# Filler matmuls at the seams between the stages of a six-stage kernel (1 core, Trainium2)

## Chip, cores and metric

The kernel is one program on one core of a Trainium2 chip. The metric is the device time of one execution in microseconds (us). A matmul engine (TensorE, PE in the profile), a vector engine (VectorE, DVE), an activation engine (ScalarE, ACT), a general engine (GpSimd, POOL) and a queue for transfers (SyncE, SP) run their own instruction streams and wait for one another by semaphores.

## What is computed

The input is 256 tokens of 1024 features in float32. Six stages follow one another, each needing the whole result of the one before. In the reference, cut to its skeleton:

```python
# first block: two layers, residual factor DN_ALPHA, layer norm after each sum
h = layer_norm(DN_ALPHA * h + mixer_ab(h, ...), ln_g[0, 0], ln_b[0, 0])    # stage ab
h = layer_norm(DN_ALPHA * h + peer(h, ...), ln_g[0, 1], ln_b[0, 1])        # stage peer0
h = layer_norm(DN_ALPHA * h + mixer_c(h, ...), ln_g[1, 0], ln_b[1, 0])     # stage c
h = layer_norm(DN_ALPHA * h + peer(h, ...), ln_g[1, 1], ln_b[1, 1])        # stage peer1
# second block: 16 meta tokens are put ahead, RMS norm ahead of each part
h = h + hybrid_mixer(rmsnorm(h, g_mix), ...)                               # stage s
h = h + peer_ffn(rmsnorm(h, g_ffn), ...)                                   # stage peer2
out = rmsnorm(h, g_final)
```

A `peer` stage scores 8 heads of product keys, picks 16 of 16384 experts per head and token, and sums the chosen experts. The kernel does this densely: it multiplies all experts and weighs them with a gate matrix.

## The kernel before

**Tiling and staging.** All weights stream from memory as slabs of 128 x 1024 float32 (512 KB) through a ring of three buffers (`ring`). ScalarE copies a slab to a rounded high part (`w_hi`, line 771), and GpSimd or VectorE subtracts to get the low part (`w_lo`, line 478). TensorE then forms each product as three matmuls, high by high, low by high and high by low (lines 521 to 523). A "column" slab multiplies the transposed input `x_hi`, `x_lo` into one of three PSUM banks (`col`), 24 matmuls of 256 columns (`features`). A "row" slab adds into the four banks `acc`, 12 matmuls of 512 columns (`rows`), with its own activations `c_hi`, `c_lo`.

**The order of the work.** Every engine's program is written out by hand, one loop over the six stages, and semaphores order the engines among one another. Nothing is scheduled by a planner.

**A seam.** At the end of a stage the sums stand in `acc`. VectorE adds the residual (line 1031), centres (line 1063) and scales, with squares and roots on ScalarE (lines 828 and 811). The scaled quarters of the new `h` (a tile of 128 tokens by half of the features each) are written at line 1074 (layer norm) or line 1137 (RMS norm) and counted in the semaphore `h_part`. TensorE, in `transpose_x` (line 580), waits for each quarter and transposes it against the identity with four instructions. ScalarE copies each transposed quarter to `x_hi` (line 800), VectorE subtracts for `x_lo` (line 1015), and the next stage's first column slab begins when two quarters of `x_lo` are there (`x_ready`). Stage `s` has 16 meta tokens more, with 8 small transposes at line 586 and a last subtraction at line 1020. From the end of the last row slab to the first `h_part`, TensorE has nothing to do.

**The start.** There is no stage before `ab`: TensorE waits for the identity and for `x` (`const`, `xload`), transposes it, and waits for the first slabs. Between the first three slabs and the fourth, the queue of transfers carries the constants of stage `ab`.

Of the kernel before, what the change touches and what calls it, by code (L numbers as in the profile page):

```python
# [20 lines left out]
BF16 = mybir.dt.bfloat16  # L21
# [5 lines left out]
P = 128  # L27
# [3 lines left out]
NT = T // P  # L31
# [43 lines left out]

PARTS_OF = {"ab": ("in", "wide", "out"), "c": ("in", "wide", "gate", "out"), "s": ("in", "gate", "conv", "out")}
RMS_AFTER = ("s", "peer2")
STAGES = ("ab", "peer0", "c", "peer1", "s", "peer2")
STAGE_OF = {f"{x}_{part}": x for x in ("ab", "c", "s") for part in ("in", "wide", "gate", "conv", "out")} | {
    f"{x}{n}": f"peer{n}" for x in ("wq", "u", "v") for n in range(3)}  # L80
# [229 lines left out]
def view(t, at, *shape, p=P):  # L310

    n = int(np.prod(shape))
    v = t[0:p, at:at + n]
    if len(shape) == 1:
        return v
    names = "abcd"[:len(shape)]
    sizes = dict(zip(names[1:], shape[1:], strict=True))
    return v.rearrange(f"p ({' '.join(names)}) -> p {' '.join(names)}", **sizes)
# [195 lines left out]
class Tensor:  # L514
# [45 lines left out]
    def rows(self, s, y_hi, y_lo, start, stop):  # L560
# [8 lines left out]
                                         skip_group_check=True)  # L569
        ins.then_inc(k.used, 1)  # L570

    def transpose_x(self, src, meta, parts):

        k, pe = self.k, self.pe
        for t in range(NT):
            for half in range(2):
                if parts:
                    pe.wait_ge(k.h_part, parts - 4 + 2 * t + half + 1)
                for c in range(4):
                    ins = pe.transpose(k.acc[t * 2 + half][:, c * P:(c + 1) * P],  # L580
                                       src[t][:, (4 * half + c) * P:(4 * half + c + 1) * P], k.ident[:, :])
                ins.then_inc(k.xt, 1)
        if meta is not None:
            self.w.next(k.meta_ready)
            for c in range(DC):
                ins = pe.transpose(k.misc[:, c * META:(c + 1) * META], meta[:, c * P:(c + 1) * P],
                                   k.ident[0:META, 0:META])
            ins.then_inc(k.xt, 1)
# [145 lines left out]
def tensor_program(k, pe):  # L734
    e = Tensor(k, pe)
    pe.wait_ge(k.const, 32)
    pe.wait_ge(k.xload, 16 * NT)
    for name in k.stages:
        if name == "s" or k.after_s(name):
            src = [view(k.big, NORMED + t * D, D) for t in range(NT)]  # L740
        else:
            src = [k.h[:, t, :] for t in range(NT)]
        meta = view(k.big, NORMED + 2 * D, D, p=META) if name == "s" else None
        e.transpose_x(src, meta, k.parts_before(name))
        if name == "s":
            e.w.next(k.x_ready, 5)
        if name[:4] == "peer":
            e.peer(int(name[4]))
        else:
            MIXERS[name](k).tensor(e)  # L750
# [5 lines left out]
class Scalar:  # L756
# [87 lines left out]
    def finish(self, name, end):  # L844
# [8 lines left out]
        self.split_lead(Slab(end))  # L853
        if name in RMS_AFTER:
            for t in range(NT):
# [509 lines left out]
def vector_program(k, dve):  # L1365
# [7 lines left out]
    for name in k.stages:  # L1373
# [7 lines left out]
        else:  # L1381
            MIXERS[name](k).vector(e)
            last = k.first[f"{name}_out"] + k.count[f"{name}_out"] - 1
        if name in RMS_AFTER:
            e.finish_rms(name, last)
# [1128 lines left out]
def build(nc, dram, out, stages):  # L2514
    with ExitStack() as ctx:
        k = Kernel(nc, ctx, dram, out, stages)
        block = ctx.enter_context(nc.Block())

        @block.sync
        def _(sp):  # L2520
            sync_program(k, sp)

        @block.gpsimd
        def _(pool):
            gpsimd_program(k, pool)

        @block.scalar
        def _(act):
            scalar_program(k, act)

        @block.tensor
        def _(pe):
            tensor_program(k, pe)

        @block.vector
        def _(dve):
            vector_program(k, dve)
# [96 lines left out]
```

## Time and profile before

| | |
|---|---|
| time, median of 3 executions | 3044.0 us (3039.75 to 3045.32) |
| the profiled execution's own time | 3041.95 us |
| its span, first to last instruction | 3040.2 us |
| mean TensorE clock granted | 0.986 of full |
| PE busy | 2950.7 us (97%) |
| DVE, ACT, POOL busy | 69%, 52%, 31% |
| bytes moved | 508.62 MB, mean 167 GB/s |

The span is what the profile's positions refer to; the time of an execution is a little longer than its span (1.75 us here). The granted clock is 1.0 where TensorE runs at 2.4 GHz and 0.5 where it runs at 1.2 GHz.

### The profile page before, as it was taken

To read this page: it belongs to the slowest core of one execution; us is meant where nothing else is said; L and a number is where in the kernel's file an instruction comes from. 1 tells how busy PE (TensorE), PEld (TensorE's weight loads), DVE (VectorE), ACT (ScalarE), POOL (GpSimd) and SP (SyncE) were. 2 spreads that over 40 slices of the span, in tenths; PEclk is the share of its full clock that TensorE was granted. 3 is DMA by queue.
4 is the path that set the end of the run, shared out by engine and by line. 5 is a ranking of instruction groups with operands and counts; after the bars stand their busy time and mean duration, and the time that the engine had idled before them with its cause. 6 is when DMAs were issued, how large, how long until landed. Compare 5 with 4: busy or idle time off the path is not lost.

```text
span 3040.2 us, 66263 instructions
## 1 busy us (share of the span) xinstructions
PE 2950.7 (97%) x22893; PEld 2687.5 (88%) x22893; DVE 2086.7 (69%) x4319; ACT 1580.0 (52%) x2614; POOL 940.8 (31%) x378
## 2 busy tenths in 40 slices
PE   7899999999999989999999999899999999999998
PEld 6799999888888879999998888788799999988887
DVE  4369488888555654948888865575429488788755
ACT  3444444677555444444457755564544444477654
POOL 5589600000004747980000000155779820000000
PEclk9999999999999999999999999899999999999999
DMA  5455555555664425555555566444555555555554
GB/s 189 141 171 180 180 159 165 166 166 166 219 193 158 139 92 172 186 184 157 164 167 166 166 213 195 142 132 125 152 161 179 187 166 160 169 161 166 186 193 159
DMA packets 142701, 508.62 MB, mean 167 GB/s; under 512 B 17136, under 2 KB 18160, under 8 KB 142592
## 3 DMA queue, kind: packets, MB, share of 16 engines
q1 hardware_dynamic: 142592, 507.16, 52.2%
q8 instruction: 69, 1.13, 0.2%
q14 instruction: 40, 0.33, 0.0%
HBM read 506.05 MB, written 1.05 MB: 167 GB/s over the span
## 4 chain that ended last, share of the span: by engine, by line
PE 87%; DVE 6%; ACT 3%; POOL 2%; issue 1%; DMA 1%; SPq 0%; DVEq 0%; ACTq 0%; POOLq 0%
PE col L521 14%; PE col L523 14%; PE col L522 14%; PE acc L521 13%; PE acc L523 12%; PE acc L522 12%; POOL w_lo L478 2%; PE acc L644 2%; PE col L644 2%; ACT w_hi L771 1%; PE acc L604 1%; DMA ring<-in_ab_in 1%; DVE work L1829 0%; DVE mask_i L1271 0%; ACT work L828 0%
## 5 line engine op out<-in xcount | busy, mean ns | idle before, releaser
L478 POOL TENSOR_TENSOR w_lo<-ring,w_hi 128x1024 fp32r<-128x1024 f32 x374 | 940.6, 2525 | 1509.6 <-ACT w_hi L771 1508.8
L771 ACT ACTIVATE w_hi<-ring 128x1024 fp32r<-128x1024 f32 x941 | 993.5, 1056 | 558.8 <-PE acc L523 460.3
L521 PE MATMUL col<-x_hi,w_hi 128*128 128x256 f32 (+1 forms) x3976 | 1133.4, 285 | 13.4 <-DVE x_lo L1015 8.7
L522 PE MATMUL col<-x_lo,w_hi 128*128 128x256 f32 (+1 forms) x3976 | 1122.6, 282 | 0.0
L523 PE MATMUL col<-x_hi,w_lo 128*128 128x256 f32 (+1 forms) x3976 | 1121.8, 282 | 0.0
L478 DVE TENSOR_TENSOR w_lo<-ring,w_hi 128x1024 fp32r<-128x1024 f32 x567 | 693.3, 1223 | 263.6 <-ACT w_hi L771 262.3
L521 PEld LDWEIGHTS col<-x_hi,w_hi 128*128 128x128 f32 x3976 | 754.7, 190 | 18.2 <-issue 12.9
L523 PEld LDWEIGHTS col<-x_hi,w_lo 128*128 128x128 f32 x3976 | 755.6, 190 | 0.0
L522 PEld LDWEIGHTS col<-x_lo,w_hi 128*128 128x128 f32 x3976 | 752.1, 189 | 0.7
L521 PE MATMUL acc<-w_hi,c_hi 128*128 128x512 f32 x1664 | 662.1, 398 | 10.6 <-DVE c_lo L1155 8.7
L523 PE MATMUL acc<-w_hi,c_lo 128*128 128x512 f32 x1664 | 651.1, 391 | 0.0
L522 PE MATMUL acc<-w_lo,c_hi 128*128 128x512 f32 x1664 | 649.9, 391 | 0.0
L778 ACT ACTIVATE work<-col 128x256 f32 (+1 forms) x464 | 178.8, 385 | 774.3 <-PE col L523 774.3
L521 PEld LDWEIGHTS acc<-w_hi,c_hi 128*128 128x128 f32 x1664 | 313.8, 189 | 76.6 <-DVE c_lo L1155 9.8
L523 PEld LDWEIGHTS acc<-w_hi,c_lo 128*128 128x128 f32 x1664 | 313.8, 189 | 67.7
L522 PEld LDWEIGHTS acc<-w_lo,c_hi 128*128 128x128 f32 x1664 | 314.3, 189 | 62.5
L1281 DVE TENSOR_TENSOR gated_onehot_i<-mask_i,pairs_of_gate 128x768 bf16<-128x768 bf16 x384 | 216.9, 565 | 12.2
L1162 DVE TENSOR_TENSOR c_lo<-work,c_hi 128x256 fp32r<-128x256 f32 x384 | 160.3, 419 | 1.4 <-ACT c_hi L932 1.4
L1271 DVE TENSOR_TENSOR mask_i<-iota_bf,pairs_of_i_i 128x256 bf16<-128x256 bf16 x384 | 127.1, 331 | 43.9 <-DVE gated_onehot_i L1281 41.0
L932 ACT ACTIVATE c_hi<-work 128x256 fp32r (+1 forms) x384 | 153.3, 401 | 5.9 <-DVE work L1291 5.9
L1169 DVE MAX8 work<-work 128x8 f32<-128x128 f32 (+1 forms) x144 | 35.4, 323 | 168.1 <-ACT work L888 167.8
L1276 DVE TENSOR_TENSOR onehot_i<-iota_bf,pairs_of_i_i 128x512 bf16<-128x512 bf16 x288 | 122.8, 426 | 0.0
(284 smaller groups left out, 2072.6 us busy)
## 6 DMA issues: line engine op xcount, KB each, us to landing
ring<-in_u SPq DMA_DIRECT2D x384, 512.0 KB, 3.4
ring<-in_v SPq DMA_DIRECT2D x384, 512.0 KB, 3.7
ring<-in_wq SPq DMA_DIRECT2D x48, 512.0 KB, 3.4
ring<-in_s_in SPq DMA_DIRECT2D x21, 512.0 KB, 3.7
ring<-in_c_in SPq DMA_DIRECT2D x16, 512.0 KB, 3.3
ring<-in_s_out SPq DMA_DIRECT2D x16, 512.0 KB, 3.7
ring<-in_s_gate SPq DMA_DIRECT2D x12, 512.0 KB, 3.7
ring<-in_s_conv SPq DMA_DIRECT2D x12, 512.0 KB, 3.7
```

The lines of the kernel that those rows point to most:

```text
L478: eng.tensor_tensor(k.w_lo[s.slot][:, :], k.ring[s.slot][:, :], k.w_hi[s.slot][:, :].bitcast(F32), ALU.subtract).then_inc(k.lo[s.slot], 1)
L521: pe.matmul(out, a[0], b[0], start=start, stop=False, **kw)
L522: pe.matmul(out, a[0], b[1], start=False, stop=False, **kw)
L523: return pe.matmul(out, a[1], b[0], start=False, stop=stop, **kw)
L644: ins = pe.matmul(banks[b.slot][:, t * EARLY:(t + 1) * EARLY], k.oh1[:, b.base % 2, t, :], k.oh2[:, b.base % 2, n, t, :], start=n == 0, st ...
L771: act.activation(k.w_hi[s.slot][:, :], k.ring[s.slot][:, :], ACT.Copy).then_inc(k.hi[s.slot], 1)
L778: act.activation(dst, src, func).then_inc(k.evac, 1)
L932: act.activation(k.c_hi[s.slot][:, :], act_of[:, s.index(values), :], ACT.Copy).then_inc(k.coef_h, 1)
L1162: dve.tensor_tensor(k.c_lo[s.slot][:, :], src, k.c_hi[s.slot][:, :].bitcast(F32), ALU.subtract).then_inc(k.coef[s.slot], 1)
L1271: dve.tensor_tensor(mask, pairs[:, at // 2:(at + EARLY) // 2, :].unsqueeze(1).to_broadcast(shape), k.i2[:, tokens, :].unsqueeze(2).to_broa ...
L1276: dve.tensor_tensor(k.oh1[:, slot, :, :].rearrange("p t (i two) -> p t i two", two=2), pairs.unsqueeze(1).to_broadcast(shape), k.i1[:, tok ...
L1281: dve.tensor_tensor(k.oh2[:, slot, :, :, :].rearrange("p n t (i two) -> p n t i two", two=2), mask.unsqueeze(1).to_broadcast(shape), k.gat ...
```

## The change

A new method issues `n` matmuls of the identity by itself, read as bf16 (256 bf16 columns of a 128 x 128 float32 tile), into the bank `col[2]`, which no one reads before it is written again. They wait for nothing and nothing waits for them. A table gives how many stand before and after the transposes of each stage. Once per program the wait for `x` moves behind the first group.

```diff
+BUSY = {"ab": (24, 50), "peer0": (40, 0), "c": (40, 0), "peer1": (40, 0), "s": (80, 0), "peer2": (20, 0)}
...
+    def keep_busy(self, n):
+
+        k = self.k
+        ones = k.ident[:, :].bitcast(BF16)
+        for _ in range(n):
+            self.pe.matmul(k.col[2][:, 0:2 * P], ones[:, 0:P], ones, start=True, stop=True)
+
...
     pe.wait_ge(k.const, 32)
-    pe.wait_ge(k.xload, 16 * NT)
     for name in k.stages:
...
+        before, after = BUSY[name]
+        e.keep_busy(before)
+        if name == k.stages[0]:
+            pe.wait_ge(k.xload, 16 * NT)
         e.transpose_x(src, meta, k.parts_before(name))
+        e.keep_busy(after)
```

On TensorE, at the seam from `ab` to `peer0`, the program before has the last row slab's matmuls, then the 16 transposes, then the first column slab (`acc` are the row banks, `c_hi` and `c_lo` the row activations):

```order
L522 MATMUL acc<-w_lo,c_hi 128x512
L523 MATMUL acc<-w_hi,c_lo 128x512
L580 MATMUL acc<-ident,h_tok 128x128 x16
L521 MATMUL col<-x_hi,w_hi 128x256
L522 MATMUL col<-x_lo,w_hi 128x256
```

and the changed program has, at the same place (all lines are numbered one to eight higher there, so 521 is now 522 and 580 is 588):

```order
L523 MATMUL acc<-w_lo,c_hi 128x512
L524 MATMUL acc<-w_hi,c_lo 128x512
L578 MATMUL col<-ident 128x256 x40
L588 MATMUL acc<-ident,h_tok 128x128 x16
L522 MATMUL col<-x_hi,w_hi 128x256
```

Only the row of line 578 is new; it stands behind the last real matmul and ahead of the transposes that wait for `h_part`. The seams into `c` and `peer1` read the same. On TensorE at the very start of the changed program:

```order
L578 MATMUL col<-ident 128x256 x24
L588 MATMUL acc<-ident,h_tok 128x128 x16
L578 MATMUL col<-ident 128x256 x50
L522 MATMUL col<-x_hi,w_hi 128x256
```

Here the two new groups stand on both sides of the transposes, and before there was only the second row. Into `s` (`misc` is the bank of the meta tokens' transposes) the changed TensorE program reads:

```order
L578 MATMUL col<-ident 128x256 x80
L588 MATMUL acc<-ident,work 128x128 x16
L594 MATMUL misc<-ident,work 128x16 x8
L522 MATMUL col<-x_hi,w_hi 128x272
```

and again the first row is all that is new. The other engines' programs are unchanged.

## Rows read from the trace of the kernel before

**Rows 1.** The page's line of busy time: engine, us, share, instructions.
```profile
PE 2950.7 (97%) x22893; PEld 2687.5 (88%) x22893; DVE 2086.7 (69%) x4319; ACT 1580.0 (52%) x2614; POOL 940.8 (31%) x378
```

**Rows 2.** Waits of TensorE: waiting line <- releaser: total us, times, longest.
```profile
PE acc L580 <- DVE h_tok L1074: 15.0, 3, 5.0
PE acc L580 <- DVE work L1137: 14.7, 4, 9.9
PE col L521 <- DVE x_lo L1015: 8.7, 5, 4.5
```

**Rows 3.** Windows at the layer-norm seams: stretch, length, busy PE PEld DVE ACT POOL, clock, DMA.
```profile
112.15:117.16 5.01, 0.00 (x1) 0.00 (x1) 4.82 (x12) 3.23 (x9) 0.00 (x0) 0.99 0.17 66
117.16:121.49 4.33, 3.58 (x17) 3.31 (x17) 3.52 (x7) 2.86 (x6) 2.37 (x1) 0.61 0.24 39
121.49:124.49 3.00, 3.00 (x25) 3.00 (x26) 1.05 (x2) 0.84 (x1) 2.09 (x1) 1.00 0.57 206
943.27:948.27 5.00, 0.00 (x1) 0.00 (x0) 4.81 (x12) 3.23 (x9) 0.00 (x0) 0.83 0.20 81
948.27:952.60 4.33, 3.67 (x16) 3.31 (x17) 3.52 (x7) 2.77 (x6) 2.37 (x1) 0.50 0.13 15
952.60:956.78 4.18, 4.18 (x19) 4.18 (x20) 3.43 (x7) 2.87 (x4) 2.38 (x1) 0.50 0.30 114
1124.39:1128.71 4.32, 3.43 (x16) 3.22 (x17) 3.51 (x7) 2.99 (x6) 2.37 (x1) 0.65 0.25 38
```

**Rows 4.** Windows at the seams into s and peer2; two timeline rows into peer2.
```profile
1949.54:1959.93 10.39, 0.45 (x2) 0.03 (x2) 8.71 (x22) 8.13 (x21) 4.63 (x3) 0.69 0.18 57
1959.93:1966.75 6.82, 4.91 (x25) 4.07 (x25) 5.23 (x12) 4.47 (x12) 0.47 (x1) 0.50 0.43 144
1966.75:1970.54 3.79, 3.79 (x17) 3.79 (x17) 0.40 (x3) 0.00 (x0) 0.00 (x0) 0.50 0.00 0
2201.84:2208.49 6.65, 3.64 (x16) 2.63 (x17) 4.02 (x9) 5.82 (x13) 3.20 (x2) 0.56 0.14 39
2208.49:2212.88 4.39, 4.39 (x20) 4.39 (x21) 1.05 (x2) 0.00 (x0) 1.49 (x1) 0.50 0.71 236
...
2201.84 1.68 PE L580 MATMUL acc<-ident,work 128*128 128x128 f32 x8 [2.65 <-DVE work L1137]
...
2206.05 2.06 ACT L800 ACTIVATE x_hi<-acc 128x512 fp32r<-128x512 f32 x4
```

**Rows 5.** Timeline: 24 gate matmuls in bf16 and 12 transposes, both at full clock.
```profile
391.52 0.87 PE L644 MATMUL acc<-gated_onehot_i,onehot_i 128*128 128x64 bf16 x24
...
1089.18 1.53 PE L1730 MATMUL col<-ident,work 128*128 128x128 f32 x12 [0.83 <-ACT work L778]
```

**Rows 6.** Timeline of the seam from ab to peer0: start, us, instruction, idle before.
```profile
117.16 3.58 PE L580 MATMUL acc<-ident,h_tok 128*128 128x128 f32 x16 [5.01 <-DVE h_tok L1074]
121.49 0.36 PE L521 MATMUL col<-x_hi,w_hi 128*128 128x256 f32 x1 [0.75 <-DVE x_lo L1015]
...
117.87 1.41 DVE L1074 SCALAR_TENSOR_TENSOR h_tok<-acc,small,work 128x512 f32<-128x512 f32 x2
120.65 1.89 DVE L1015 TENSOR_TENSOR x_lo<-acc,x_hi 128x512 fp32r<-128x512 f32 x3 [0.78 <-ACT x_hi L800]
```

**Rows 7.** Timeline of GpSimd at the start of stage c (the fourth slab).
```profile
959.04 2.40 POOL L478 TENSOR_TENSOR w_lo<-ring,w_hi 128x1024 fp32r<-128x1024 f32 x1 [3.06 <-ACT w_hi L771]
```

**Rows 8.** Start of stage ab: TensorE's first slab and fourth slab, and a window.
```profile
15.13 0.55 PE L521 MATMUL col<-x_hi,w_hi 128*128 128x256 f32 x1 [4.54 <-DVE x_lo L1015]
25.99 0.35 PE L521 MATMUL col<-x_hi,w_hi 128*128 128x256 f32 x1 [0.80 <-POOL w_lo L478]
...
16.00:17.00 1.00, 1.00 (x7) 1.00 (x7) 0.18 (x1) 0.00 (x0) 1.00 (x1) 0.50 1.06 414
```

**Rows 9.** Windows inside stage ab: a wait, and the matmuls behind it.
```profile
76.97:79.00 2.03, 0.02 (x1) 0.00 (x0) 0.00 (x0) 1.97 (x3) 1.66 (x2) 1.00 0.45 182
79.00:82.00 3.00, 2.89 (x15) 2.89 (x16) 0.52 (x1) 2.43 (x4) 1.51 (x1) 0.59 0.63 198
```

## The prediction

> **What bounds the kernel now.** I read four views, from coarse to fine. The page's busy line says that TensorE works 97% of the span [rows 1], so what can be won lies in its few waits and in stretches at half clock. The view of waits then names them: the transposes at the head of a stage wait 15.0 us over three layer-norm seams and 14.7 us over the RMS-norm seams, and first slabs wait 8.7 us for `x_lo` [rows 2]. All of these are waits for VectorE and ScalarE, which filler matmuls don't shorten. The windows show the clock. In the 5.0 us without a matmul before each layer-norm seam's transposes the granted clock falls from full (2.4 GHz) to half (1.2 GHz), at the very end of the wait into `peer0` (mean 0.99) and earlier into `c` (mean 0.83). Then the transposes run at half clock, and into `c` so do the first 19 matmuls of the stage, up to 956.78 [rows 3]. The RMS-norm seams look worse: 3.79 us of half-clock matmuls into `s` and 4.39 us into `peer2` [rows 4]. So the kernel loses, besides the waits, some microseconds per seam to a slow clock, and that alone is what the change can reach.
>
> **What the fillers cost.** The trace has no 256-column bf16 matmul. From above: 24 gate matmuls of 64 bf16 columns with their weight loads take 0.87 us, 0.036 us each [rows 5], and 192 columns more at 2.4 GHz add 0.080, which makes 0.116 us. The fp32r matmuls of 256 columns take 3.00 / 25 = 0.12 us each at full clock [rows 3]. From below: 256 columns at 2.4 GHz are 0.107 us. I take 0.116. At half clock it is twice the columns' time, 0.213 at least (19 fp32r matmuls in 4.18 us are 0.22 [rows 3]). So 40 fillers last 4.6 us against a wait of 5.0 us [rows 3], 80 last 9.3 us against 10.4, and 20 last 2.3 us against 2.65 [rows 4]. The fillers end before `h_part` comes by 0.4, 1.1 and 0.3 us, so they cost nothing themselves. The cover is thin: a layer-norm seam pays every nanosecond by which one filler exceeds 0.125 us.
>
> **A layer-norm seam, step by step** (into `peer0`; the others read alike). With the clock kept up, four transposes take 4 x 1.53 / 12 = 0.5 us instead of 0.9 [rows 5, 6]. Transposes also wait for each quarter of `h`. VectorE writes the third and fourth from 117.87 on in 1.41 us, so the third is there at about 118.6. Its transposes end at 119.1 instead of about 120.0, ScalarE's copy (0.6 us) ends at 119.7, and VectorE, which waited 0.78 us for it before 120.65 [rows 6], no longer waits. The first slab waits for that subtraction, so it starts 0.78 us earlier. That is all that the transposes' speed gives: of 1.8 us saved on TensorE, the rest was behind VectorE's own pace anyway. Into `peer0` and `peer1` the clock of the profiled execution had already risen within the transposes (means 0.61 and 0.65, and 1.00 behind them [rows 3]), so these two seams give 0.8 us each.
>
> **Into c** there is more. 19 matmuls at half clock take 4.18 us [rows 3], and at 0.12 us they take 2.3: 1.9 us less. Late next is the fourth slab. GpSimd finishes its low part at 959.04 + 2.40 = 961.44 [rows 7]. The chain of small operations behind it on VectorE and ScalarE starts from the same `x_lo`, so it moves up by 0.78 too, to 960.66. TensorE would be through three slabs at 951.82 + 72 x 0.12 = 960.46 and waits 0.2 us. The seam gives 0.8 + 1.9 - 0.2 = 2.5 us.
>
> **Into s and peer2** the fillers cover only the first wait. Behind it lie 6.82 us and 6.65 us until the first slab, in which TensorE at half clock is busy 4.91 and 3.64 us [rows 4], and at full clock about half of that, with pauses near 2 us between the bursts. Does the clock last through? Inside stage `ab` it fell within the matmuls that followed a single wait of 2.0 us (mean 0.59 over 79 to 82 [rows 9]). So here it falls again, before the first slab or just behind it, and it comes back as late as now. Into `peer2` the transposes' speed does not matter either: ScalarE copies all four quarters in one go from 2206.05 [rows 4], after its own slab work. I give `peer2` nothing and `s` 0.3 us for faster transposes in its last tile.
>
> **At the start** the 24 fillers ahead (5.1 us at half clock) lie in the wait for `x`, and what they might push back ends at the same place as the rest. The 50 behind the transposes last 5.8 us at full clock against a wait of 4.54 us: the first slab would start 1.3 us late. In return it does not run at half clock (0.50 at 16 to 17 us [rows 8]), which is worth about 14 x 0.1 = 1.4 us. And whatever is won or lost here meets the fourth slab, which comes from a transfer behind the constants; TensorE waits 0.80 us for it at 25.99 [rows 8]. Net 0. Should all 50 run at half clock (10.7 us, 6.1 late), 0.8 us of that is hidden and some 4 us are lost.
>
> **The sum.** 0.8 + 2.5 + 0.8 + 0.3 + 0 + 0 = 4.4 us. The profiled execution took 3041.95 us, so 3037.6. That execution is 2 us below the median of 3044.0, and I do not add these 2 us back. Where the clock rises behind a layer-norm seam changes between three seams of the same program: within the transposes at two, 4.18 us into the matmuls at the third [rows 3]. So it is chance per seam, worth 0 to 1.9 us, and slower executions of the kernel before plausibly lost it at more seams. With fillers no seam depends on it. Against the median the gain is then 4.4 + 2.0 = 6.4 us.
>
> **The rule that speaks against this.** The row first: between 112.15 and 121.49 the only instructions of TensorE are the 16 transposes, and the clock rises while they run (mean 0.61 from 117.16, full behind) [rows 3], so transposes do raise the clock. The Trainium skill, "TensorE: Matmul & The Clock Gate", Part 4, says that the clock gate does not engage for transpose-mode matmuls, which don't count as busy the same way. By that rule the fillers' effect would lapse before the first slab, and the sum would be near 0; the trace disagrees with it.
>
> **The rivals.**
> - *The clock lapses within the transposes* (the rule above, as a mechanism of this kernel). At full clock the transposes are busy 1.8 of 4.3 us, much thinner than the dense 3.58 us of now. If the clock falls about when the first slab begins, each of three seams keeps 0.8 us and runs some 4 us of matmuls slowly, which costs 1.9. Into `peer0` and `peer1` that is new (+1.1 each), into `c` it is what stands now (-0.8). With `s` it sums to +1.1: 3043. For it: the single wait of 2.0 us that sufficed in [rows 9]. Against it: the longest pause in these seams would be about 0.9 us. Chance 0.15.
> - *The change does not do what it says*: the identity read as bf16 is nearly all zeros, and if that doesn't hold the clock, all is as before, 3040 to 3045. Against it: the gate matmuls, on one-hot operands nearly all zeros too, run through at full speed [rows 5]. Chance 0.10.
> - *It holds everywhere*: `s` and `peer2` also keep their clock, which gives 3.79 x 0.45 + 4.39 x 0.45 = 3.7 us more: 3034. Chance 0.12.
> - *The fillers outlast the wait* (the one that ends slower). Its place is ahead of the transposes: TensorE runs in order, so `h_part` arrives and finds it multiplying the identity. Each filler beyond 0.125 us delays three seams by 40 x the excess and `s` by 80 x the excess over 0.130. It eats the gain of 4.4 us at about 0.15 us per filler (3.0 + 1.6 us) and gives 3050, 0.2% above the median, at about 0.18 us. At half clock, 0.213, it would be 3.5 us at three seams and 6.6 at `s`: 3055. For it: margins of 0.4 us on a price that the trace only bounds. Against it: both bounds are below 0.125. Chance 0.05.
>
> The forecast has the remaining 0.58.
>
> **How the numbers follow.** A measurement of this kernel can tell about 0.2% (6 us) from no change. The forecast, 3037.6, stands at the edge of that against 3044.0, so it splits nearly evenly between faster and the same; the case of all seams is faster, the two without effect are the same, and the last is half slower. Faster 0.58 x 0.55 + 0.12 + a little = 0.45; slower 0.04; same 0.51. The range takes in the full hold, 3034, with the executions' own scatter of about 1 us below, and the two cases without gain up to 3043. The forecast's own range is 3035 to 3040.
>
> **What would show it.** In the profile after: the fillers at 0.107 to 0.12 us each; clock 1.00 through the layer-norm seams; each of these seams' first matmul 0.8 us sooner after the last row matmul; VectorE's 0.78 us wait before `x_lo` gone; clock 0.5 still in the first slabs of `s` and `peer2`; the wait for the fourth slab in `ab` longer than 0.80 us. Wrong would be a half clock in the first slab of `peer0`, `c` or `peer1`, or transposes that start with no wait behind the fillers.

## Result and the profile after

| | kernel before | changed kernel |
|---|---|---|
| median of 10 runs each, us | 3040.73 | 3046.47 |
| lowest to highest, us | 3036.16 to 3045.32 | 3040.64 to 3051.51 |
| profiled execution, us | 3041.95 | 3046.23 |

The ratio is 1.0022 with a 95% interval of 1.0012 to 1.0033: the changed kernel is slower by 0.2%, some 6 us. I had forecast 3037.6 us and a gain, and had given 0.04 to slower. Both kernels scatter by 9 to 11 us from run to run, which matters for all that follows.

The page of the changed kernel, TensorE's busy line and the queue that brings the instructions of the long programs (packets, MB, share of the DMA engines' time):

```profile
PE 2978.3 (98%) x23187; PEld 2708.2 (89%) x23187; DVE 2090.1 (69%) x4319; ACT 1580.2 (52%) x2614; POOL 941.9 (31%) x378
...
q8 instruction: 71, 1.16, 0.2%
```

Against [rows 1] there are 23187 - 22893 = 294 matmuls more, and nothing else of size. Queue 8, whose packets are of 16 KB, had 69 packets in the kernel before.

TensorE's waits in the changed kernel (who waits <- releaser: total us, times, longest):

```profile
PE acc L652 <- DVE gated_onehot_i L1293: 7.3, 3, 4.3
PE col L522 <- POOL w_lo L479: 6.7, 7, 2.3
PE col L522 <- DVE x_lo L1027: 5.0, 4, 2.5
PE acc L588 <- DVE work L1149: 4.8, 4, 1.6
PE acc L588 <- DVE h_tok L1086: 2.4, 6, 0.6
```

And the two of them that had been smaller in the kernel before:

```profile
PE acc L644 <- DVE gated_onehot_i L1281: 4.7, 3, 1.6
PE col L521 <- POOL w_lo L478: 3.4, 6, 1.3
```

The waits of [rows 2] shrank as they should (15.0 to 2.4, 14.7 to 4.8, 8.7 to 5.0 us; the rest is now fillers). Two others grew: for the gates in the peer stages (4.7 to 7.3 us) and for GpSimd's low part of the weights (3.4 to 6.7 us).

The windows at the layer-norm seams and into `s` and `peer2` (stretch, length, busy PE PEld DVE ACT POOL, granted clock, DMA share, GB/s):

```profile
118.28:121.95 3.67, 2.62 (x17) 1.70 (x17) 3.51 (x7) 2.95 (x6) 2.36 (x1) 1.00 0.13 26
...
948.50:952.18 3.68, 2.62 (x16) 1.71 (x17) 3.52 (x7) 2.95 (x6) 2.38 (x1) 1.00 0.00 0
952.18:956.00 3.82, 3.82 (x32) 3.82 (x33) 3.44 (x4) 2.02 (x2) 2.41 (x1) 1.00 0.41 137
...
1962.73:1969.55 6.82, 4.25 (x25) 3.34 (x25) 5.24 (x12) 4.47 (x12) 0.48 (x1) 0.68 0.40 129
1969.55:1973.00 3.45, 3.45 (x15) 3.45 (x16) 0.39 (x3) 0.00 (x0) 0.00 (x0) 0.50 0.03 5
...
2206.77:2213.42 6.65, 2.62 (x17) 1.71 (x17) 4.02 (x9) 5.82 (x13) 3.20 (x2) 1.00 0.16 39
2213.42:2218.00 4.58, 4.58 (x26) 4.58 (x27) 1.05 (x2) 0.00 (x0) 1.49 (x1) 0.63 0.72 224
```

Beside [rows 3], the transposes and the first slab of the layer-norm stages now run at clock 1.00 (2.4 GHz), and from the first transpose to the first slab it takes 3.67 us instead of 4.33. Into `s` that stretch is 6.82 us as in [rows 4] and the first slab runs at half clock again (0.50), and into `peer2` it is 6.65 us, also as in [rows 4], although the transposes there now run at full clock. So the fillers do hold the clock where I said, and the stretch is shorter where I said. The time is lost elsewhere.

The timeline of TensorE (start, us, what, and in brackets the wait ahead) at the start, into `peer0`, at the fourth slab of `c` and into `s`:

```profile
3.48 5.30 PE L578 MATMUL col<-ident 128*128 128x256 bf16 x24 [3.48 <-DMA work<-in_iota]
8.58 2.29 PE L588 MATMUL acc<-ident,h_tok 128*128 128x128 f32 x16
10.70 5.62 PE L578 MATMUL col<-ident 128*128 128x256 bf16 x50
16.08 0.36 PE L522 MATMUL col<-x_hi,w_hi 128*128 128x256 f32 x1
...
113.11 4.54 PE L578 MATMUL col<-ident 128*128 128x256 bf16 x40
118.28 0.44 PE L588 MATMUL acc<-ident,h_tok 128*128 128x128 f32 x2 [0.62 <-DVE h_tok L1086]
...
963.23 0.35 PE L522 MATMUL col<-x_hi,w_hi 128*128 128x256 f32 x1 [2.29 <-POOL w_lo L479]
...
1952.63 8.91 PE L578 MATMUL col<-ident 128*128 128x256 bf16 x80
1962.73 0.66 PE L588 MATMUL acc<-ident,work 128*128 128x128 f32 x4 [1.20 <-DVE work L1149]
```

40 fillers take 4.54 us and end 0.62 us before the transposes can start. At the fourth slab of `c` stands a wait of 2.29 us that the kernel before did not have.

**Where the time went.** I set every real matmul of one trace against the same one of the other, since both programs have the same 22893. Into `peer0`, the shorter stretch is there. In `c`, the changed kernel is 2.3 us ahead of the kernel before by the fourth slab, where the wait of 2.29 us takes all of it back. The largest step is in `peer1`: between 1342 and 1380 us the changed kernel loses 4.5 us, with no filler near. A smaller one, 2 us near 2000 and 2015 us in stage `s`, is not there in a second profile of the same program (e1 below). Here are the rows. Behind the routing transposes (line 634) the sync engine issues the 512 KB transfer of a slab. Its issue and the time to landing, and a packet of queue 8 found between 1344.2 and 1344.5, in the changed kernel:

```profile
q8 instruction: 1, 0.02, 25.3%
...
ring<-in_u SPq DMA_DIRECT2D x1, 512.0 KB, 5.0
```

the same transfer in the kernel before, where the packet of queue 8 comes at 1350.1, 2.7 us after the transfer has landed:

```profile
ring<-in_u SPq DMA_DIRECT2D x1, 512.0 KB, 3.1
```

What then follows on ScalarE, VectorE, GpSimd and TensorE, in the timelines of the changed kernel:

```profile
1347.75 1.06 ACT L783 ACTIVATE w_hi<-ring 128x1024 fp32r<-128x1024 f32 x1 [1.25 <-DMA ring<-in_u]
1348.72 0.36 ACT L929 ACTIVATE neg_i<-misc 128x256 f32<-128x256 f32 x1
...
1354.16 2.51 DVE L1265 TENSOR_TENSOR gated_onehot_i<-gated_onehot_i,pairs_of_gate 128x256 f32<-128x256 f32 x1
...
1367.21 0.55 DVE L1293 TENSOR_TENSOR gated_onehot_i<-mask_i,pairs_of_gate 128x768 bf16<-128x768 bf16 x1
...
1348.89 12.59 POOL L479 TENSOR_TENSOR w_lo<-ring,w_hi 128x1024 fp32r<-128x1024 f32 x5 [1.71 <-ACT w_hi L783]
...
1367.81 0.39 PE L652 MATMUL acc<-gated_onehot_i,onehot_i 128*128 128x64 bf16 x4 [4.32 <-DVE gated_onehot_i L1293]
```

its window behind the wait:

```profile
1367.81:1370.00 2.19, 2.19 (x19) 2.19 (x20) 1.61 (x5) 0.00 (x0) 0.00 (x0) 0.51 0.68 239
```

and in the kernel before:

```profile
1348.99 0.38 ACT L917 ACTIVATE neg_i<-misc 128x256 f32<-128x256 f32 x1
...
1354.80 0.42 DVE L1253 TENSOR_TENSOR gated_onehot_i<-gated_onehot_i,pairs_of_gate 128x256 f32<-128x256 f32 x1
...
1349.17 2.40 POOL L478 TENSOR_TENSOR w_lo<-ring,w_hi 128x1024 fp32r<-128x1024 f32 x1 [0.34 <-ACT w_hi L771]
1352.08 2.41 POOL L478 TENSOR_TENSOR w_lo<-ring,w_hi 128x1024 fp32r<-128x1024 f32 x1 [0.50 <-ACT w_hi L771]
...
1366.55 0.44 PE L644 MATMUL acc<-gated_onehot_i,onehot_i 128*128 128x64 bf16 x9 [1.42 <-DVE gated_onehot_i L1281]
```

Read it as a chain. The transfer lands 1.9 us later. ScalarE works in order and waits 1.25 us for it, and the small copy `neg_i` stands behind that slab: counted from the routing transposes (1342.4 and 1344.1 us) it starts at +6.3 instead of +4.9. Now GpSimd has five slabs to do in a row (12.59 us) instead of one or two at a time with pauses of 0.3 to 0.7 us between, and the operation of VectorE that took 0.42 us in such a pause takes 2.51 us beside it. So the gates come 2.9 us later, TensorE waits 4.32 us instead of 1.42, and in that pause its clock falls (0.51 over the next 2.19 us). One 16 KB packet of instructions at the wrong moment costs 4.5 us.

That was the theory after the result: **the fillers cost through the instructions that they add.** 294 matmuls are 588 instructions of TensorE, and where in the program queue 8 fetches its next block moves with their number. The rivals were that the fillers cost something by running (power, banks, a wait that they outlast), or that 6 us is chance between executions. The Trainium skill, "Runtime: NRT & Kernel Launch", section "Instruction fetch mechanics", says that each engine's sequencer fetches its instructions itself in blocks of 16 KB (256 instructions) over a DMA queue of its own, and that crossing a block's boundary is mostly hidden. The size agrees with the trace (1.16 MB / 71 packets). That it is hidden agrees for TensorE itself, whose idle time put down to issue is 0.7 us in all; it does not hold for the transfer beside it.

### The profile page after: what moved, and what is told of

The parts are those of the page before. It is cut to its first block, busy times and chain, and to the rows that moved or that the text cites. A ratio compares the mean times of both kernels' runs of the same rounds, so it can differ in the third digit from the quotient of the medians.

```text
span 3044.4 us, 66850 instructions
## 1 busy us (share of the span) xinstructions
PE 2978.3 (98%) x23187; PEld 2708.2 (89%) x23187; DVE 2090.1 (69%) x4319; ACT 1580.2 (52%) x2614; POOL 941.9 (31%) x378
## 3 DMA queue, kind: packets, MB, share of 16 engines
q8 instruction: 71, 1.16, 0.2%
## 4 chain that ended last, share of the span: by engine, by line
PE 86%; DVE 6%; ACT 3%; POOL 3%; issue 1%; DMA 1%; SPq 0%; ACTq 0%; DVEq 0%; POOLq 0%
PE col L522 14%; PE col L524 14%; PE col L523 14%; PE acc L522 13%; PE acc L524 12%; PE acc L523 12%; POOL w_lo L479 3%; PE acc L652 2%; PE col L652 2%; ACT w_hi L783 1%; PE acc L612 1%; DMA ring<-in_ab_in 1%; DVE work L1841 0%; DVE mask_i L1283 0%; ACT work L840 0%
## 5 line engine op out<-in xcount | busy, mean ns | idle before, releaser
L522 PEld LDWEIGHTS col<-x_hi,w_hi 128*128 128x128 f32 x3976 | 754.1, 190 | 17.3 <-issue 11.7
```

The lines of the kernel that those rows point to most:

```text
L522: pe.matmul(out, a[0], b[0], start=start, stop=False, **kw)
```

## Experiments

The thirteen traces answer more than their times, so here is one table ahead. For each peer stage: when the fetch of queue 8 starts, counted from the first routing transpose; when the slab transfer issued at +0.2 lands; when ScalarE's `neg_i` starts; what TensorE waits for gates in the stage; and the time from the first routing transpose to the 300th matmul behind it (all us, worked out from the traces' records).

| kernel, stage | fetch | landed | neg_i | gate waits | 300 matmuls |
|---|---|---|---|---|---|
| before, peer0 | +1.2 | +4.50 | +5.55 | 1.62 | 33.1 |
| before, peer1 | +6.0 | +3.33 | +4.93 | 1.42 | 32.9 |
| changed, peer0 | +1.18 | +4.28 | +5.33 | 1.37 | 32.9 |
| changed, peer1 | +1.84 | +5.25 | +6.30 | 4.32 | 37.4 |
| changed again, peer0 | +1.5 | +5.15 | +6.20 | 4.20 | 37.9 |
| changed again, peer1 | +2.17 | +5.30 | +6.35 | 4.37 | 37.9 |
| e3, peer0 | +1.18 | +4.32 | +5.37 | 1.64 | 33.2 |
| e3, peer2 | +1.28 | +5.20 | +6.25 | 4.26 | 37.2 |
| e5, peer0 | +1.47 | +4.68 | +5.73 | 3.96 | 37.6 |
| e5, peer1 | +2.09 | +5.35 | +6.40 | 4.27 | 37.5 |
| e6, peer0 | +1.18 | +4.44 | +5.49 | 1.65 | 33.2 |
| e6, peer1 | +1.78 | +4.94 | +5.99 | 4.15 | 37.7 |
| e7, peer0 | +1.24 | +4.53 | +5.58 | 1.63 | 33.1 |
| the other 26 | +3.5 and later | +3.3 to +3.7 | +4.9 | 1.35 to 1.63 | 32.9 to 33.2 |

Two remarks. The effect is a step: up to `neg_i` at +5.58 nothing is lost, from +5.73 on 4 to 5 us are, in seven of the 39 stages. The kernel before stands close to the step itself, in its `peer0`, so it may pay in some of the executions that were not profiled; that is not shown. And the late landing is one sixteenth of the transfer. A transfer counts up its semaphore sixteen times, once for each of the 16 DMA engines. In all twelve stages with a fetch at +1.2 to +2.2, fifteen of the sixteen counts are there by +3.3 to +3.7, as in a stage without a fetch, and one alone comes at +4.3 to +5.35.

Each experiment was timed against the kernel before on its own chip; that one's median was 3037.61 us for the first four runs, 3037.60 for the next four and 3040.71 for the last three.

**The changed kernel again** (e1).

> The changed kernel once more, unaltered. In its first profile it lost 4.5 us at one place outside the seams: the wait for the gated one-hots in stage peer1 was 4.32 us where the kernel before had 1.42, and the clock fell behind it. Theory A (that place is chance, and the seams give back what they win): the wait is back at 1.4 to 1.6 us here, the span is 3040 to 3042, and over the rounds the ratio is below 1.002. Theory B (the long wait belongs to the change, because stages start sooner and meet transfers and GpSimd in another phase): the wait is above 3 us again, the span near 3044, ratio 1.002 or more.

3047.72 us, ratio 1.0035 [1.0022, 1.0047]. So it is slower on a second chip too, and both intervals lie above 1. In its profiled execution the collision stands in two stages, `peer0` and `peer1`; in the first profile of the same program `peer0` had escaped it, with its fetch 0.3 us earlier against the transposes.

**The layer-norm seams alone** (e2).

```
-BUSY = {"ab": (24, 50), "peer0": (40, 0), "c": (40, 0), "peer1": (40, 0), "s": (80, 0), "peer2": (20, 0)}
+BUSY = {"ab": (0, 0), "peer0": (40, 0), "c": (40, 0), "peer1": (40, 0), "s": (0, 0), "peer2": (0, 0)}
```

> Fillers at the three layer-norm seams alone (40 each; none at the start, at s and at peer2). Theory A: each seam's first matmul comes 0.7 us sooner, the fourth slab of stage c waits above 2 us and takes c's gain back, so the time is 1 to 3 us below the kernel before. Theory B: the wait for the gated one-hots of peer1 is above 3 us and the time is 3 to 6 us above the kernel before. Theory C (the harm is at s and peer2): as A.

3034.16 us, ratio 0.9989 [0.9980, 0.9998]: 3.5 us faster than before, with the same fillers at the same seams as in the changed kernel. None of its three peer stages has a fetch before +7.9.

**s and peer2 alone** (e3): 80 fillers into `s`, 20 into `peer2`, none elsewhere.

> Fillers at the seams into s and peer2 alone (80 and 20). Theory A: no gain and no loss, within 1 us of the kernel before, since the clock falls behind the fillers anyway and the transposes are paced by VectorE. Theory C (the fillers there move the fall of the clock into the matmuls of stage s, whose half-clock stretches in the changed kernel were 1970 to 1975 and 2012 to 2016): 3 to 5 us above the kernel before. Theory B: as A.

3043.24 us, ratio 1.0019 [1.0009, 1.0028]. No gain at these seams, and a loss of 5.6 us between the medians. The profile shows 4.1 of it in `peer2`, where the fetch fell on +1.28 (+11.5 in the kernel before). That execution took 3037.39 us, one of the two fastest of twelve, so what the slower ones lost beside it is not seen.

**The start alone** (e4): 24 and 50 fillers in `ab`.

> Fillers at the start alone (24 and 50). All theories but one expect nothing, within 1 us: the fourth slab of stage ab waits for its transfer (1.04 us in the changed kernel). Theory D (the start moves the phase of everything that follows, above all of the chip's clock decisions, and the program's other waits happen to lie badly for it): 2 us or more above the kernel before.

3042.05 us, ratio 1.0013 [1.0004, 1.0021]. Slower, and no peer stage of its profile has a collision. Here the theory of the number fell short, and e10 below takes it up.

**All 294, each a quarter as wide** (e5). The instructions and their places are those of the changed kernel, but with 64 columns each TensorE is idle for most of every wait.

```
-            self.pe.matmul(k.col[2][:, 0:2 * P], ones[:, 0:P], ones, start=True, stop=True)
+            self.pe.matmul(k.col[2][:, 0:P // 2], ones[:, 0:P], ones[:, 0:P // 2], start=True, stop=True)
```

> All 294 fillers of the change, at the same places, but each of 64 columns: about 0.036 us each, so 40 last 1.4 us and don't hold the clock, while the program has exactly as many instructions. The traces show 16 KB instruction fetches whose place in the program moves with the fillers' number; where one falls 1.1 to 2.2 us behind the routing transposes of a peer stage, the slab transfer there lands at +4.3 to +5.3 us instead of +3.3 and the wait for the gates grows from 1.4 to up to 4.4 us. Theory C (instruction volume): fetches at peer0 +1.2 to +1.5 and peer1 +1.8 to +2.2 as in the changed kernel, a gate wait above 4 us at peer1, and a ratio of 1.002 to 1.005, since the layer-norm seams' gain is gone too. Theory E (the harm is in what the fillers execute): within 0.1% of the kernel before.

3045.37 us, ratio 1.0025 [1.0016, 1.0034]. A loss of this size is there while the fillers' work is down to a fraction: the added instructions alone are enough for it. That is not the same loss part by part, since the seams' gain and the start's cost are gone too. TensorE's largest waits in this kernel:

```profile
PE acc L588 <- DVE work L1149: 12.1, 4, 7.6
PE acc L588 <- DVE h_tok L1086: 11.5, 3, 3.8
PE acc L652 <- DVE gated_onehot_i L1293: 9.9, 4, 4.0
```

The first two are the seams' waits, nearly as long as in [rows 2]; the third holds the collisions in `peer0` and `peer1`, 4.5 us each by the table, 9 in sum against a measured 7.8.

**40 and then 74 short fillers at one seam** (e6, e7). The kernel before, with nothing added but short fillers into `peer1`:

```
+BUSY = {"ab": (0, 0), "peer0": (0, 0), "c": (0, 0), "peer1": (40, 0), "s": (0, 0), "peer2": (0, 0)}
```

and (74, 0) in the second.

> The kernel before with 40 fillers of 64 columns (1.4 us in a wait of 5.0) at the seam into peer1 alone. They move the fetch of peer1 from +6.0 to about +1.9 us. Theory C: slab landed at +4.3 to +5.3, gate wait above 4 us at peer1 and a half-clock stretch behind it, 3 to 5 us above the kernel before (ratio 1.001 to 1.0015). Theory E: gate wait 1.4 us, ratio 1.000.

> As e6_pad40 but with 74 fillers of 64 columns (2.7 us, still inside the wait): nearly twice the instructions. The fetches of peer1 and peer2 then lie at about +13 and +3.5 us, outside the harmful stretch. Theory C: gate waits 1.4 and 1.6 us, ratio within 0.0007 of 1, so less harm than with 40. A theory by which harm grows with the number of instructions expects more than in e6_pad40.

With 40: 3040.77 us, ratio 1.0009 [0.9999, 1.0019]. With 74: 3039.54 us, ratio 0.9998 [0.9990, 1.0007]. The times alone hardly separate the two. The traces do. The 33 us behind the routing transposes of `peer1`, with 40:

```profile
1343.60:1376.60 33.00, 28.85 (x245) 28.69 (x244) 22.17 (x22) 12.43 (x19) 22.52 (x10) 0.90 0.46 160
```

and with 74:

```profile
1342.20:1375.20 33.00, 31.63 (x304) 31.43 (x303) 25.74 (x31) 14.24 (x23) 22.48 (x10) 1.00 0.51 176
```

304 matmuls at clock 1.00 against 245 at 0.90, and the clean one is the kernel with *more* added instructions. The fetch behind `peer1`'s routing transposes moved from +6.0 to +1.8 with 40 fillers. With 74 no fetch is near: the last one ahead is at 1194.8 us, and the next comes at +13.4. These are single traces, but they tell the place of a fetch from the number of instructions as such.

**The changed kernel with its fetches moved** (e8). The fillers of the layer-norm seams, of `s` and the first 24 stay. The start's 50 become 90 short ones, and `peer2`'s 20 become 108 short ones, so that no fetch falls between +0.2 and +3 in a peer stage.

```
-BUSY = {"ab": (24, 50), "peer0": (40, 0), "c": (40, 0), "peer1": (40, 0), "s": (80, 0), "peer2": (20, 0)}
+BUSY = {"ab": (24, 0), "peer0": (40, 0), "c": (40, 0), "peer1": (40, 0), "s": (80, 0), "peer2": (0, 0)}
+MOVED = {"ab": (0, 90), "peer2": (108, 0)}
...
+        e.keep_busy(MOVED.get(name, (0, 0))[0], P // 2)
         e.transpose_x(src, meta, k.parts_before(name))
         e.keep_busy(after)
+        e.keep_busy(MOVED.get(name, (0, 0))[1], P // 2)
```

> The changed kernel with its fetches moved: the 50 fillers behind the first transposes become 90 of 64 columns, and the 20 of peer2 become 108 of 64 columns, so that peer0 and peer1 see 40 fillers' instructions more ahead of them and peer2 128 more, one fetch in all. Layer-norm seams and s keep their full fillers. Theory C: no fetch between +0.2 and +3 us at any of the three peers, gate waits 1.4 to 1.6 us, 5 to 9 us below the changed kernel and at or below the kernel before (ratio 0.998 to 1.001). Theory E: as the changed kernel, 1.002 to 1.0035.

3036.68 us, ratio 0.9993 [0.9984, 1.0002], with fetches at +11.7, +8.7 and +5.9. It has 128 fillers more than the changed kernel, and by the ratios (1.0022 and 1.0035, on other chips) it is 9 to 13 us faster. The start also changed in this kernel, so not all of that is the fetches'.

**Is c worth its fillers?** (e9, with e11). e9 is e2 with the 40 fillers of `c` 64 columns wide; e11 is e2 once more, as its companion.

```
-        e.keep_busy(before)
+        e.keep_busy(before, P // 2 if name == "c" else 2 * P)
```

> The fillers of the layer-norm seams alone, and those of stage c with 64 columns each in place of 256: the same instructions at the same places, but TensorE idles through most of c's wait. If what the fillers win at c is all given back at its fourth slab (a wait of 2.3 us there, in the place of 19 matmuls at half clock), the profile shows half clock behind c's transposes and no wait at the fourth slab, and the time is within 1 us of the kernel with all three seams held, next to it in the same comparison. The rival, that c is worth the 2.5 us of my sum: 2.5 us slower than that kernel.

> The kernel with the 3 x 40 fillers of the layer-norm seams alone, once more, as the companion of the one with c's fillers short. It measured 0.9989 [0.998, 0.9998]; if that was more than luck it comes out at 0.9985 to 0.9995 again, with all gate waits of the peer stages below 1.7 us. The rival, luck: 0.9997 or more.

e11: 3037.22 us, ratio 0.9986 [0.9976, 0.9996], so the gain of the three seams stands (3.5 us between the medians both times). e9: 3039.86 us, ratio 0.9998 [0.9989, 1.0006], 2.6 us more than e11, though the intervals overlap. By my expectation that is the rival's number, and the trace is not as I expected either. Its windows over the transposes of `c`, the first three slabs, the wait for the fourth, and a stretch behind it:

```profile
945.74:950.06 4.32, 3.40 (x16) 3.19 (x17) 3.51 (x7) 3.01 (x6) 2.37 (x1) 0.65 0.09 28
950.06:958.50 8.44, 8.43 (x71) 8.44 (x72) 5.81 (x9) 4.81 (x7) 2.39 (x1) 1.00 0.34 112
958.50:961.03 2.53, 0.29 (x3) 0.10 (x2) 0.00 (x0) 2.40 (x4) 2.49 (x2) 1.00 0.00 0
...
962.50:965.80 3.30, 3.30 (x17) 3.30 (x17) 0.00 (x0) 0.38 (x2) 3.05 (x2) 0.50 0.72 242
```

The clock had come back within the transposes this time, so the first slabs ran at full clock without the fillers' help, met the fourth slab's wait (2.25 us), and the clock fell behind that wait. The fourth slab starts 14.7 to 14.8 us behind the first transpose in the kernel before and in all five traces with full fillers at `c`, and 14.4 to 15.3 in the seven others without. What delays it where the clock is full is shown under "Into c" below. The 414th matmul from the first transpose comes at +54.9 to +55.0 in four of those five and at +56.5 in one, and at +54.6 to +57.0 (mean 55.5) in the eight without. By these records full fillers at `c` win 0.3 us on average; by the times of e9 and e11 they could win up to 2.6. Both are within what chance does here, and this stays open.

**The start with short fillers** (e10): e4 with 64 columns each.

> The 74 fillers of the start alone, with 64 columns each. The same 74 with 256 columns measured 3042.05 us, ratio 1.0013, with every gate wait of the peer stages short. If what costs there is the added instructions (the fetch that moves from 26 to 18 us, in between the transfers of the constants), this is the same, 1.001 to 1.002. If it is TensorE's time, 50 full fillers that outlast the wait for the first slab, it is gone: 0.999 to 1.0003, and the first slab starts at 14 to 15 us.

3039.86 us, ratio 1.0000 [0.9991, 1.0009], with its first fetch at 17.7 us, close to e4's (18.3). By the expectation it is not the number but TensorE's time, though the two intervals overlap and the two were timed on different chips. TensorE's timeline at the start, e4 first:

```profile
4.15 5.28 PE L578 MATMUL col<-ident 128*128 128x256 bf16 x24 [4.15 <-DMA work<-in_iota]
9.24 1.93 PE L588 MATMUL acc<-ident,h_tok 128*128 128x128 f32 x16
```

and e10:

```profile
6.75 3.67 PE L588 MATMUL acc<-ident,h_tok 128*128 128x128 f32 x16 [2.26 <-DMA h_tok<-in_x]
...
13.99 0.38 PE L522 MATMUL col<-x_hi,w_hi 128*128 128x256 f32 x1 [1.89 <-DVE x_lo L1027]
...
25.46 0.36 PE L522 MATMUL col<-x_hi,w_hi 128*128 128x256 f32 x1 [1.21 <-POOL w_lo L479]
```

The wide fillers outlast both waits: in e10 `x` is there at 6.75 while in e4 the transposes start at 9.24, and the first slab, which in e10 starts at 13.99, starts at 16.39 in e4. But nothing of that is left at the fourth slab. e10 waits 1.21 us for it and starts it at 25.46, e4 runs its first slabs at full clock and starts it at 24.99, with no wait, and the kernel before starts it at 25.99 [rows 8]. By the first transpose of `peer0` e4 is 1.1 us behind e10 and 0.6 us behind the kernel before (117.72 against 116.64 and 117.16), and at the end of the span 0.6 us behind the kernel before. So the 4.4 us between the medians of e4 and the kernel before (0.0013 of the time by the ratio) are not placed: the profiled executions don't show them at the start or anywhere else.

## Why the prediction was wrong

**The step that failed** is the sentence "The fillers end before `h_part` comes by 0.4, 1.1 and 0.3 us, so they cost nothing themselves." The margins were right. But I asked only what the fillers do while they run, and left out the term for what they are: 588 instructions that have to be fetched, and whose fetches meet the transfers of the slabs. That term is 4.0 to 5.0 us for each peer stage in which a fetch starts +1.3 to +2.2 us behind the routing transposes. The changed kernel pays it in `peer1` in both profiles, and in `peer0` in one of two. None of my four rivals named it, and the slower side had 0.04 for all causes together.

**What the fillers cost.** I took 0.116 us each; 4.54 / 40 = 0.114 and 8.91 / 80 = 0.111 were measured. They outlast none of the five later waits (0.62, 0.61, 0.60, 1.20 and 0.45 us are left). Right. A slip in the rival of outlasting fillers: at 0.18 us per filler its own terms give 120 x 0.055 + 80 x 0.050 = 10.6 us and 3048; the 3050 that it names belong to about 0.19. It changes no chance.

**A layer-norm seam.** Clock 1.00 through all three: right, in every profile with full fillers there. 0.78 us sooner: 4.33 - 3.67 = 0.66 us, in all 17 such seams of the thirteen traces (3.67 or 3.68), against 4.13 to 4.33 in the 22 without. VectorE's wait of 0.78 us is gone: four subtractions now follow in one row,

```profile
120.31 2.69 DVE L1027 TENSOR_TENSOR x_lo<-acc,x_hi 128x512 fp32r<-128x512 f32 x4
```

so that step was right and its size 0.1 us too large. What I undervalued is `peer1`. In five of seven traces without full fillers there, the clock was still half behind the first slab for some 4 us, as in this row of e3:

```profile
1121.20:1125.10 3.90, 3.90 (x18) 3.90 (x19) 1.05 (x2) 0.93 (x1) 2.37 (x1) 0.51 0.45 156
```

which costs about 2 us more; in all six with them it was 1.00. I had read one trace, where the clock had come back in time, and had put this to chance "worth 0 to 1.9 us". (That it was 1.00 behind `peer1`'s transposes I gave as [rows 3], which end before; the trace does have it.) Into `peer0` it did not happen in any of seven.

**Into c.** Here the term was mis-sized: I had TensorE wait 0.2 us for the fourth slab, and it waits 2.29 to 2.34 us in all five traces. The step that failed is "it moves up by 0.78 too, to 960.66". I let the chain of small operations keep its length, and it got longer. The changed kernel, GpSimd and VectorE:

```profile
952.99 2.41 POOL L479 TENSOR_TENSOR w_lo<-ring,w_hi 128x1024 fp32r<-128x1024 f32 x1 [1.68 <-ACT w_hi L783]
...
953.15 2.27 DVE L1817 TENSOR_TENSOR work<-work 128x8 f32<-128x8 f32 x1
```

and the kernel before:

```profile
953.60 2.38 POOL L478 TENSOR_TENSOR w_lo<-ring,w_hi 128x1024 fp32r<-128x1024 f32 x1 [2.54 <-ACT w_hi L771]
...
953.57 0.16 DVE L1805 TENSOR_TENSOR work<-work 128x8 f32<-128x8 f32 x1
```

The first small operation, 8 elements wide, took 0.16 us when it started 0.03 us ahead of GpSimd's subtraction, and takes 2.27 us when it starts 0.16 us behind it. Those 2.1 us pass down the chain: counted from the first transpose, GpSimd ends the low part of the fourth slab at +14.6 instead of +13.2, where +12.4 was forecast. It is the same in all thirteen traces. In seven the first slabs of `c` run at full clock, GpSimd starts first, the small operation takes 2.1 to 2.3 us and TensorE waits 2.1 to 2.3 us for the fourth slab (e4 and e9 among them, without full fillers at `c`). In the other six the first ones run at half clock, the operation takes 0.16 us and there is no wait. So TensorE's faster slabs win nothing. Of 2.5 us forecast, 0 to 0.3 are seen in the traces (and up to 2.6 in one pair of times).

**The sum of the three** was 4.1 us, and e2 and e11 measured 3.5 each. That agreement is partly luck: `c` gave less and `peer1` more than their terms.

**s and peer2.** Right in the main: the first slab into `s` is at half clock (0.50), the one into `peer2` mostly (a mean of 0.63 over 4.58 us, 0.50 over 4.39 before), and nothing is gained in `peer2`. Its transposes do run at full clock (1.00), and it brings nothing, since the first slab waits for ScalarE and VectorE, as I had it. The 0.3 us for `s` are not in the changed kernel's first profile (6.82 us to the first slab, as before), but in the three others with its 80 fillers (6.50, 6.35 and 6.37).

**At the start** I had net 0. The full-width fillers hold back the first slab, 16.08 us instead of 15.13. I had the 1.3 us that the 50 outlast the wait, but not that the 24 (5.3 us at half clock, from 3.48 on) outlast the one for `x`; I had written that "what they might push back ends at the same place". In the traces it does end at the same place: the fourth slab starts at 25.88 us in the changed kernel and at 25.99 in the kernel before. The wait for it is longer in the changed kernel's first profile, 1.04 us against 0.80, as forecast, but e1 and e4, with the same start, have none. By the times the term was not 0 but 4.4 us (e4), and where they are lost stays open.

**The rule on transposes** that I weighed (the Trainium skill, "TensorE: Matmul & The Clock Gate", Part 4: the clock gate does not engage for transposes) was rightly set aside for this kernel: the clock rises within the transposes with the last filler 3.82 us ahead of them (e9, 0.65 over 945.74 to 950.06 and 1.00 behind), and behind the fillers the transposes of the three seams run at 1.00 throughout, with 2.62 us busy in 3.67, and the slabs behind them too.

**The ledger** in medians: three seams -3.5, the start +4.4 (e4), one collision +4.5, a second one in some executions up to +4.6. That makes 5.4 to 10.0 us, against 5.7 and 10.1 us measured in the two comparisons. The sum comes out, but not every term of it is explained: the start's share is a difference of medians that no profile shows, and how often the second collision happens is known from two profiles alone.

## What to carry to other kernels

An instruction that does nothing useful still has to be fetched, and on a kernel whose transfers are tight the question is not how many instructions are added but which transfer the next block of instructions then meets. So after such a change look first at the stages that it did not touch, and compare two versions that differ by instructions alone (short dummies in the place of long ones) before giving a price to what the instructions do.

A faster engine also shifts when its neighbours meet. At the seams where a slab's data was ready the fillers gave 0.7 us and a safe clock. In `c` they brought GpSimd's subtraction just ahead of a small operation of VectorE that TensorE's fourth slab depends on, instead of just behind it, and lost there what they had won. And one trace shows one draw of a clock that comes back early or late; the same seam should be read in several.

## What was not expected of the hardware

- A fetch of 16 KB of instructions that starts 1.0 to 1.9 us after a 512 KB transfer on 16 DMA engines was issued made that transfer land 4.4 to 5.1 us after its issue instead of 3.1. A 16 KB packet is 1/32 of its bytes. Fifteen of the transfer's sixteen counts come in time and one alone is late, which fits one DMA engine whose share waits behind the packet.
- Some of VectorE's operations take 2.1 to 2.6 us when they start while a GpSimd operation runs, whatever their own size: 2.51 us instead of 0.42 for 256 elements, and 2.27 instead of 0.16 for 8. In `peer1` this turned 1.4 us of delay into 2.9, and in `c` it took back the whole gain.
- Another two-way draw: the first wait of a later part of stage `ab` (TensorE for VectorE's pool mixer) is 4.74 us in eight traces and 2.2 to 2.5 in five, of the same program too (the changed kernel has the one in its first profile and the other in its second). Stage `peer0` then starts at 115.7 to 118.3 us in the eight and at 111.2 to 115.1 in the five, and this may be much of the scatter of 9 to 13 us. In the eight the mixer's last two operations of VectorE take 2.5 and about 3.3 us; in each of the five one of them takes 0.4 or 1.2. What decides which stays open.
